# A chunk's picks within 30 slots instead of 36, and the dense gates spread over 108 slots instead of 72

## The chip, the cores and the metric

The kernel runs on one core of a Trainium2 chip. The metric is the device time of one execution in microseconds (us), lower is better. The kernel before takes 3666.66 us, the median of three runs (3649.32 to 3670.26 us).

## The reference

The program is one layer of a decoder. Its first half mixes tokens with two recurrent head groups and ends in a first layer norm. The second half, which this case is about, is PEER: each token picks 16 of 16384 experts for each of 8 heads and sums their outputs.

```
s = einsum('thcd,hckd->thck', q, keys)          # two score lists of 128 keys for each head
s1, i1 = top_k(s[:, :, 0], 16);  s2, i2 = top_k(s[:, :, 1], 16)
cand = s1[..., :, None] + s2[..., None, :]      # 256 sums, whose best 16 are the picks
top, pos = top_k(cand, 16)
eidx = take_along_axis(i1 * 128 + i2, pos);  gate = softmax(top)
hid = gelu(einsum('td,thkd->thk', x, u[eidx]))
out = einsum('thk,thkd->td', gate * hid, v[eidx])
x2 = LayerNorm(ALPHA * x1 + out)
```

There are 1024 prompt tokens in 8 chunks of 128, and 8 sample tokens that are padded to a ninth chunk. All data are float32.

## The kernel before, in words

The function `build_peer` writes out by hand the order of the instructions of each of the five engines as one loop over 656 slots (`for t in range(SLOTS)`). The engines are tied by semaphores alone.

Five chunks (0 to 4) are gathered: a slot t brings the row of `peer_u` of one pick of each of the 128 tokens with an indirect DMA of GpSimd (L1437, 512 KB), and VectorE forms the dot product of it with the token (L1707, "the dot"). 20 slots later the row of `peer_v` of the same pick is gathered in the same way (L1437) and TensorE adds it into PSUM (L2053), with gates that ScalarE writes as diagonals (L1893). So a slot is two gathers of 512 KB, one dot, and half a pair of v rows on TensorE. There are four buffers for u rows and four for v rows. GpSimd issues the gather of slot t once the dot of slot t - 4 is done. The number of a slot is the number of its dot, and the windows of the trace that stand below are cut at the starts of dots.

Three chunks (5, 6, 7) are dense. Their gates are spread into a matrix of 16384 experts by 384 tokens in DRAM, and from slot 320 (`SD`) on 128 blocks of experts are multiplied whole on TensorE (L2002, L2013, L2026), beside the rest of the gathers. Block b has its place at slot 321 + 13b/5.

Beside the slots below 320 runs the preparation of the chunks, in the order 0, 1, 5, 6, 2, 7, 3, 4, sample. `background(s)` says in which period q a slot lies and at which place `at` in it. Below slot 24 q is 0. From there a period has 36 slots: q = 1 from slot 24, q = 7 from slot 240, q = 8 in slots 276 to 311. In a period q:

- VectorE does `pick(q, ...)` in 22 steps (two lots of four heads with 11 steps each), and `norm1` of chunk q+1 in 6 steps. Four steps of a lot are `top16` over four lists of score sums of 128 keys together (L1530 to L1545), two are `top16` over 80 sums, two are the three wide operations L1596, L1600 and L1601, and the other three are short.
- TensorE does the output projection `mix` of chunk q+2 in 16 steps (L1971, two matmuls each), the transposes of chunk q+1 (L1980) and its 32 `score` steps (L1989). Before, one mix step stands in each slot from 2 to 12 and from 31 to 35, and two score steps in each slot from 15 to 30.
- ScalarE takes roots and exponentials, copies scores and the transposed chunk out of PSUM, and issues the stores of `x1`, of the transposed dense chunk and of the picks.
- The queue of SyncE loads four pieces of 256 KB of `mixT` (`load_mt`), 512 KB of `x` (`load_x`) and every 16 slots turns a set of gates (`turn_gates`). It works strictly in order, so a wait of one load holds the later ones.

The spreading of the dense gates is done in 96 quads of four tokens. A quad is four `tensor_scalar` (L1652) and one `tensor_tensor` (L1654) of VectorE that make one-hot rows, four small matmuls (L2096), and a copy by ScalarE to the tile `stag` (L1856). Every eighth quad a store of 2 MB to `gd_d` follows. Before, the quads stand in slots 246 to 317, four in three slots (`quad_slot`). The picks of the three dense chunks are transposed just ahead of them, in slots 243 to 246. They use PSUM banks 2 and 3, which the last `mix` must have left.

After slot 320 ScalarE waits with its first copy for the last quad and for all stores to `gd_d`.

Of the kernel before, what the change touches and what calls it, by code (L numbers as in the profile page):

```python
# [1067 lines left out]
def build_peer(nc, a, o, L_):  # L1068
# [12 lines left out]
    GATHERED, DENSE, SAMPLE = 5, (5, 6, 7), 8  # L1081
    ORDER = (0, 1, 5, 6, 2, 7, 3, 4, 8)
    PICK = {t: p for p, t in enumerate(ORDER)}
    NP = len(ORDER)
    ND = len(DENSE)
# [2 lines left out]
    U_SLOTS = GATHERED * CH  # L1088
    LAG, LAG_PE, SD = TOPK, TOPK + 4, 320
    PE_ROWS = SD - LAG_PE  # L1090
    SLOTS = U_SLOTS + LAG
    NBLK = NE // P
    GQ = TD // 4
# [9 lines left out]

    def background(s):

        return (0, s) if s < 24 else ((s + 12) // 36, (s + 12) % 36)

    def v_rows(t):

# [11 lines left out]
    def by_dve(v):  # L1121

        return max(0, v - PE_ROWS)

# [2 lines left out]
        return 2 * p + 2 if p else 0  # L1127

    def quad_slot(q):
        return 246 + q * 72 // GQ  # L1130

    def block_slot(b):
        return SD + 1 + b * 13 // 5
# [5 lines left out]
    with ExitStack() as ctx:  # L1139
# [103 lines left out]
        with nc.Block() as block:  # L1243
            @block.sync
            def _(sp):
# [96 lines left out]
                for t in range(SD):  # L1342
                    q, at = background(t)
                    p = q + 1
                    if at == 0 and q + 2 < NP:
                        load_mt(q + 2, 1)
                    if at == 6 and q + 2 < NP:
                        load_mt(q + 2, 2)
                    if at == 10 and q + 2 < NP:
                        load_mt(q + 2, 3)  # L1350
                    if at == 15 and p + 1 < NP:
                        load_x(p + 1)
                    if (t == 22 or at == 32) and q + 3 < NP:
                        load_mt(q + 3, 0)
                    if t in (1, 8, 15, 23):
                        load_first_gixv(t // 7)
                    if t == 64:
                        load_gix(1)
                        load_gixv(1)
                        load_x1g(1)  # L1360
                    if t == 172:
                        sp.wait_ge(s["ysum"], 1)
                        load_gix(2)
                        load_gixv(2)
                    if t == 242:
                        sp.wait_ge(s["mixg"], 4 * NP - 3)
                        for d in range(ND):
                            sp.wait_ge(s["pkst"], 16 * PICK[DENSE[d]])
                            sp.dma_start(pkd[:, d, :, :], pk_d[DENSE[d], :, 0:3, :]).then_inc(s["pkl"], 16)
                        load_x1g(2)  # L1370
                    if t == 254:
                        sp.wait_ge(s["x1"], NP)
                        wide(gb1[:, :], "ln2_g", s["gl1"])
                        wide(gb2[:, :], "ln2_b", s["gl2"])
                    if t == 274:
                        sp.wait_ge(s["sco"], 4 * NP)
                        for d in range(ND):
                            sp.wait_ge(s["xtst"], 16 * (d + 1))
                            sp.dma_start(xraw[:, :, d * CH:(d + 1) * CH], xt_d[d]).then_inc(s["xdl"], 16)
                    if t == 286:  # L1380
                        sp.wait_ge(s["ysum"], 2)
                        load_gix(3)
                    if t >= TOPK and t % TOPK == 0 and t // TOPK <= (PE_ROWS + TOPK - 1) // TOPK:
                        turn_gates(t // TOPK - 1)
                    if t == 300:
                        for b in range(3):
                            load_u(b)
                        for b in range(3):
                            load_v(b)
                    if t == 304:  # L1390
                        sp.wait_ge(s["stored"], 16)
                        load_x1g(3)
# [98 lines left out]
            def _(dve):  # L1491
# [195 lines left out]
                for t in range(SLOTS):  # L1687
                    c, h, k = t // CH, t % CH // TOPK, t % TOPK
                    q, at = background(t)
# [64 lines left out]
                            pick(0, 1 + step // 8, step % 8)  # L1754
                    if 1 <= q < NP:
                        for step in range(22):
                            if 1 + step * 34 // 21 == at:
                                pick(q, step // 11, step % 11)
                    norm_at = (1, 2, 3, 6, 7, 11) if q else (8, 9, 10, 12, 13, 15)
                    if q + 1 < NP and at in norm_at:  # L1760
                        norm1(q + 1, norm_at.index(at))

# [52 lines left out]
            def _(act):  # L1815
# [21 lines left out]
                def exp(p, part):  # L1837
                    nh = 4 if p else 2
                    hs = slice(nh * part, nh * part + nh)
                    act.wait_ge(s["top0"], parts_before(p) + part + 1)  # L1840
                    S.activation(gates_of(p)[:, hs, :], gates_of(p)[:, hs, :], ACT.Exp).then_inc(s["exp0"], 1)
# [39 lines left out]
                for t in range(SLOTS):  # L1881
                    q, at = background(t)
# [15 lines left out]
                    if q + 1 < NP:  # L1898
                        if at == (4 if q else 11):
                            root1(q + 1)  # L1900
                        if at == (12 if q else 16):
                            act.wait_ge(s["x1"], q + 2)
                            act.dma_start(x1_d[tok(ORDER[q + 1]), :], x1[:, :]).then_inc(s["x1st"], 16)
                        if at == (14 if q else 17):
                            evac_x1(q + 1)
                        if at == 16 and ORDER[q + 1] in DENSE:
                            act.wait_ge(s["x1tc"], q + 2)
                            act.dma_start(xt_d[DENSE.index(ORDER[q + 1])], x1T[:, :, :]).then_inc(s["xtst"], 16)
                        if t == 23 or at == 31:
                            evac_scores(q + 1, 0)  # L1910
                            evac_scores(q + 1, 1)
                    if t in (5, 12, 20):
                        exp(0, (5, 12, 20).index(t) + 1)
                    if t in (6, 8):
                        evac_scores(0, t // 2 - 1)
                    if 1 <= q < NP and at in (13, 31):
                        exp(q, at // 31)
                    for r in range(len(NORM2)):
                        if t - NORM2[r] == 3:
                            root2(r, mv7[:, 1:2])  # L1920
                        if t - NORM2[r] == 13:
                            store_y(r)
                    if t in (244, 245, 246):
                        d = t - 244
                        act.wait_ge(s["pkt"], d + 1)
                        S.copy(it[:, d, :, :].rearrange("p a n -> p (a n)"), PB[:, 2 + d % 2, 0:3 * HK]).then_inc(s["pkc"], 1)
                    for n in range(GQ):
# [35 lines left out]
            def _(pe):  # L1963
                def mix(p, j):
                    m = 4 * p + j // 4 - 3
                    if j % 4 == 0:
                        pe.wait_ge(s_mt[m % 2], 16 * (m // 2 + 1))
                    if j == 0:
                        free(pe, s["stt"], p)
                    for h in range(2):  # L1970
                        last = T.matmul(PB[:, 2 + h, :], mt[:, m % 2, j % 4, :], wo[:, j, h * 512:(h + 1) * 512], start=j == 0, stop=j == 15)  # L1971
                    if j % 4 == 3:
                        last.then_inc(s["mixg"], 1)
# [67 lines left out]
                for t in range(SD):  # L2041
                    q, at = background(t)
# [13 lines left out]
                    if q == 0:  # L2056
                        for j in range(16):
                            if 9 + j * 13 // 15 == t:
                                mix(2, j)
                        if t == 16:  # L2060
                            transposes(1)
                        if 18 <= t < 23:
                            for i in range(32 * (t - 18) // 5, 32 * (t - 17) // 5):
                                score(1, i)
                    else:
                        if q + 2 < NP:
                            if 2 <= at <= 12:
                                mix(q + 2, at - 2)
                            elif at >= 31:
                                mix(q + 2, at - 20)  # L2070
                        if q + 1 < NP:
                            if at == 13:
                                transposes(q + 1)
                            if 15 <= at <= 30:
                                score(q + 1, 2 * (at - 15))
                                score(q + 1, 2 * (at - 15) + 1)
                    if t in (243, 244, 245):
                        d = t - 243
                        if d == 0:
                            pe.wait_ge(s["stt"], NP)  # L2080
                            pe.wait_ge(s["pkl"], 16 * ND)
                        else:
                            free(pe, s["pkc"], d - 1)
                        pe.sem_inc(s["passed"], 1)
                        for x in range(3):
                            last = T.transpose(PB[:, 2 + d % 2, x * HK:(x + 1) * HK], pkd[:, d, x, :], ident[:, :])
                        last.then_inc(s["pkt"], 1)
# [117 lines left out]
```

## Time and profile before

| | |
|---|---|
| median of three runs | 3666.66 us |
| the profiled execution: own time | 3655.92 us |
| its span | 3653.9 us |
| mean granted TensorE clock | 0.949 |
| PE, DVE, ACT, POOL busy over the span | 89%, 71%, 23%, 48% |
| dot of slot 0, 24, 210, 318 starts at | 1079.7, 1161.1, 1793.3, 2273.5 us |

The page cuts the span into 40 slices of 91.3 us. Slots 24 to 318 lie in slices 13 to 25. The busy shares over the whole span say little here, since stages with different limits follow each other. One has to read the shares of each stretch.

### The profile page before, as it was taken

How to read it: one execution, taken by the hardware profiler on the slowest of the kernel's cores; microseconds unless marked ns; L12 is line 12 of the kernel's file. 1: busy time of each engine (PE TensorE's matmuls, PEld its weight loads, DVE VectorE, ACT ScalarE, POOL GpSimd, SP SyncE). 2: the span in 40 equal slices, each digit the busy share in tenths (PEclk: the TensorE clock that was granted, in tenths of full speed). 3: DMA queues.
4: the chain of work that ended last, by engine and by line, in shares of the span. 5: the costliest groups of instructions: out<-in, count | busy, mean ns of one | idle time of the engine just before them, and what ended most of it. 6: DMA issues, size and time to landing. Idle time of an engine off the chain costs nothing.

```text
span 3653.9 us, 46321 instructions
## 1 busy us (share of the span) xinstructions
PE 3256.1 (89%) x15535; PEld 2241.9 (61%) x15535; DVE 2610.8 (71%) x5599; ACT 831.4 (23%) x1727; POOL 1738.2 (48%) x1424
## 2 busy tenths in 40 slices
PE   6998999799988888888877656899999999999998
PEld 6998998789833223222324433577766766777765
DVE  6662000598847788888889998777777777877777
ACT  2111111465511111111113333111111111111111
POOL 2333220122203667666775566555555555555553
PEclk9999999899899999999999878899999999999999
DMA  3334333666755999999998888999999999999997
GB/s 102 87 85 144 111 127 105 234 235 226 281 208 176 345 344 348 347 335 348 364 334 289 297 298 298 396 391 383 394 390 394 393 385 381 377 400 393 396 374 247
DMA packets 392043, 1074.32 MB, mean 294 GB/s; under 512 B 57872, under 2 KB 155120, under 8 KB 384672
## 3 DMA queue, kind: packets, MB, share of 16 engines
q0 software_dynamic: 186624, 679.56, 50.0%
q1 hardware_dynamic: 132024, 298.86, 22.9%
q10 hardware_dynamic: 73192, 93.41, 7.1%
q8 instruction: 101, 1.65, 0.2%
q14 instruction: 102, 0.84, 0.1%
HBM read 978.45 MB, written 93.02 MB: 293 GB/s over the span
## 4 chain that ended last, share of the span: by engine, by line
PE 37%; DVE 13%; DMA 11%; issue 7%; POOL 4%; ACT 0%; POOLq 0%; DVEq 0%; SPq 0%; ACTq 0%
PE PB L2026 16%; PE PB L2013 13%; DMA vbf<-in_peer_v,gixv 6%; DMA x1d<-in_peer_u 3%; DVE ub L1707 3%; PE PB L2002 3%; DVE oha L1652 2%; PE PB L2053 2%; POOL ub L1437 2%; POOL vbf L1437 2%; DVE ohb L1654 1%; DMA ub<-in_peer_u,gix 1%; PE PB L1989 1%; PE PB L1971 1%; DVE work L1600 0%
## 5 line engine op out<-in xcount | busy, mean ns | idle before, releaser
L1437 POOL DMA_INDIRECT ub<-in_peer_u,gix x640 | 722.8, 1129 | 673.7 <-DVE hid L1707 477.9
L2026 PE MATMUL PB<-vbd,wd 128*128 128x512 f32 x1536 | 683.3, 595 | 0.0
L2013 PE MATMUL PB<-xds,uts 128*128 128x384 f32 x3072 | 568.4, 339 | 0.0
L2013 PEld LDWEIGHTS PB<-xds,uts 128*128 128x128 f32 x3072 | 530.7, 189 | 0.5 <-issue 0.5
L1437 POOL DMA_INDIRECT vbf<-in_peer_v,gix x340 | 396.1, 1165 | 163.9 <-issue 99.1
L1437 POOL DMA_INDIRECT vbf<-in_peer_v,gixv x300 | 353.4, 1178 | 252.0 <-PE PB L2053 121.6
L2026 PEld LDWEIGHTS PB<-vbd,wd 128*128 128x128 f32 x1536 | 283.2, 191 | 308.5 <-issue 308.5
L2053 PE MATMUL PB<-vbf,dg 128*64 128x512 f32 x1200 | 336.7, 686 | 131.8 <-DMA vbf<-in_peer_v,gixv 130.5
L1668 DVE TENSOR_TENSOR uts<-PB,uts 128x512 fp32r<-128x512 f32 x256 | 175.8, 687 | 295.6 <-ACT uts L1869 295.3
L1707 DVE CUSTOM_DVE_ANT_0 ub<-ub,x1g 128x1024 f32<-128x1024 f32 x257 | 313.6, 1222 | 78.4 <-DMA ub<-in_peer_u,gix 69.0
L1707 DVE CUSTOM_DVE_ANT_0 ub<-ub,x1gb 128x1024 f32<-128x1024 f32 x256 | 311.2, 1216 | 3.8 <-DMA ub<-in_peer_u,gix 3.5
L1869 ACT CAST uts<-PB 128x512 fp32r<-128x512 f32 x256 | 150.1, 586 | 644.1 <-PE PB L2002 631.9
L2053 PEld LDWEIGHTS PB<-vbf,dg 128*64 128x64 f32 x1200 | 90.0, 151 | 321.9 <-issue 309.2
L1746 DVE SCALAR_TENSOR_TENSOR acc<-vbf,wg,acc 128x1024 f32<-128x1024 f32 x212 | 271.2, 1279 | 5.2 <-DMA vbf<-in_peer_v,gix 4.0
L1989 PE MATMUL PB<-wp,x1T 128*128 128x512 f32 x576 | 269.3, 611 | 1.2 <-ACT x1T L1835 1.2
L1971 PE MATMUL PB<-wo,mt 128*128 128x512 f32 x528 | 248.3, 615 | 14.3 <-DVE x L1498 9.6
L270 PE MATMUL PB<-wtkh,xh 128*128 128x256 f32 (+1 forms) x864 | 244.5, 283 | 11.2 <-ACT xps L304 11.2
L967 DVE MEMSET onec<- 128x1 f32 x1 | 0.1, 59 | 345.8 <-PEq L108 345.8
L270 PE MATMUL PB<-wtkh,xl 128*128 128x256 f32 (+1 forms) x864 | 243.3, 282 | 0.0
L270 PE MATMUL PB<-wtkl,xh 128*128 128x256 f32 (+1 forms) x864 | 242.5, 281 | 0.0
L2096 PE MATMUL PB<-oha,ohb 128*128 128x128 f32 x768 | 131.5, 328 | 106.9 <-DVE ohb L1654 106.8
L2096 PEld LDWEIGHTS PB<-oha,ohb 128*128 128x128 f32 x768 | 114.2, 230 | 157.0 <-DVE ohb L1654 144.0
(399 smaller groups left out, 5340.0 us busy)
## 6 DMA issues: line engine op xcount, KB each, us to landing
vbd<-in_peer_v SPq DMA_DIRECT2D x128, 512.0 KB, 7.0
x1d<-in_peer_u SPq DMA_DIRECT2D x96, 512.0 KB, 9.3
gd_d<-stag ACTq DMA_DIRECT2D x12, 2048.0 KB, 10.1
gbd<-gd_d SPq DMA_DIRECT2D x16, 1536.0 KB, 19.0
ubd<-in_peer_u SPq DMA_DIRECT2D x32, 512.0 KB, 9.6
wtr<-in_w_tok SPq DMA_DIRECT2D x12, 1024.0 KB, 8.1
tok_d<-stg ACTq DMA_DIRECT2D x96, 128.0 KB, 1.7
rb<-rows_d SPq DMA_DIRECT2D x8, 1536.0 KB, 8.3
```

The costliest lines, as they stand in the source:

```text
L270: last = nc.tensor.matmul(PB[0:n, b, 0:TW], x[:, k, t * CH:t * CH + n], w[:, k, :], start=k == 0 and v == 0, stop=k == KD - 1 and v == 2)
L1437: pool.indirect_dma_start(out=buf, out_offset=None, in_=a[table], in_offset=bass.IndirectOffsetOnAxis(ap=index, axis=0)).then_inc(done, 16)
L1668: V.tensor_tensor(uts[:, b % 2, 1, 4 * x:4 * x + 4, :].rearrange("p k e -> p (k e)"), PB[:, 7, :], uts[:, b % 2, 0, 4 * x:4 * x + 4, :].re ...
L1707: V.tensor_tensor_reduce(out=ub[:, t % NB, :], in0=ub[:, t % NB, :], in1=by, scale=1.0, scalar=0.0, op0=ALU.mult, op1=ALU.add, accum_out=i ...
L1746: V.scalar_tensor_tensor(y, vbf[:, v % NB, :], wg[:, hv % 2, col:col + 1], y, ALU.mult, ALU.add).then_inc(s["ax"], 1)
L1869: S.copy(uts[:, b % 2, 0, 4 * x:4 * x + 4, :].rearrange("p k e -> p (k e)"), PB[:, 7, :]).then_inc(s["utc"], 1)
L1971: last = T.matmul(PB[:, 2 + h, :], mt[:, m % 2, j % 4, :], wo[:, j, h * 512:(h + 1) * 512], start=j == 0, stop=j == 15)
L1989: last = T.matmul(PB[:, 4 + n, :].rearrange("p (h n) -> p h n", h=4), x1T[:, kk, :], wp[:, 4 * n:4 * n + 4, kk, :], start=kk == 0, stop=kk ...
L2013: last = T.matmul(PB[:, 6, 0:TD], uts[:, b % 2, ul, k, :], xds[:, xl, k, :], start=(k, n) == (0, 0), stop=(k, n) == (KD - 1, 2))
L2026: last = T.matmul(PB[:, 2 * d + n, :], wd[:, b % 2, d * CH:(d + 1) * CH], vbd[b % 8][:, n * 512:(n + 1) * 512], start=b == 0, stop=b == NB ...
L2053: last = T.matmul(PB[64 * g:64 * g + 64, x, :], dg[:, n % 2, g, :], vbf[:, (v0 + g) % NB, x * 512:(x + 1) * 512], start=v0 % CH == 0, stop ...
L2096: last = T.matmul(PB[:, 2 + m % 2, x * P:(x + 1) * P], ohb[:, m % 2, x, :], oha[:, m % 2, x, :], start=True, stop=True)
```

## The change

The period becomes 30 slots (`PERIOD`), so q = 7 starts at slot 204, q = 8 at slot 234, and the preparation ends at slot 264. The 22 steps of a pick stand in slots 1 to 29 of a period. The steps of `norm1`, the roots, exponentials, copies, stores and loads get earlier places in it. The mix steps follow a list: one in each slot from 2 to 10, and seven in slots 25 to 29. The 32 score steps stand in slots 12 to 24, two or three in a slot. The work of slots below 24 stays as it was. The gates are spread from slot 210 (`SPREAD`) on, eight quads in nine slots, up to slot 316; what stood ahead of them (the loads of the dense picks, their transposes and copies) moves from slots 242 to 246 to slots 206 to 210, and the load of the second norm's weights from slot 254 to slot 216.

```diff
+    PERIOD, SPREAD = 30, 210
+    MIX_AT = (2, 3, 4, 5, 6, 7, 8, 9, 10, 25, 26, 26, 27, 28, 28, 29)
@@ background
-        return (0, s) if s < 24 else ((s + 12) // 36, (s + 12) % 36)
+        return (0, s) if s < 24 else (1 + (s - 24) // PERIOD, (s - 24) % PERIOD)
@@ quad_slot
-        return 246 + q * 72 // GQ
+        return SPREAD + q * (SD - 2 - SPREAD) // GQ
@@ SyncE
-                    if at == 15 and p + 1 < NP:
+                    if at == (13 if q else 17) and p + 1 < NP:
                         load_x(p + 1)
-                    if (t == 22 or at == 32) and q + 3 < NP:
+                    if (t == 22 or q and at == 27) and q + 3 < NP:
                         load_mt(q + 3, 0)
-                    if t == 242:
+                    if t == SPREAD - 4:
-                    if t == 254:
+                    if t == 216:
@@ VectorE
-                            if 1 + step * 34 // 21 == at:
+                            if 1 + step * 28 // 21 == at:
                                 pick(q, step // 11, step % 11)
-                    norm_at = (1, 2, 3, 6, 7, 11) if q else (8, 9, 10, 12, 13, 15)
+                    norm_at = (1, 2, 3, 5, 6, 9) if q else (8, 9, 10, 12, 13, 15)
@@ ScalarE
-                        if at == (12 if q else 16):
+                        if at == (10 if q else 16):
                             act.wait_ge(s["x1"], q + 2)
                             act.dma_start(x1_d[tok(ORDER[q + 1]), :], x1[:, :]).then_inc(s["x1st"], 16)
-                        if at == (14 if q else 17):
+                        if at == (12 if q else 17):
                             evac_x1(q + 1)
-                        if at == 16 and ORDER[q + 1] in DENSE:
+                        if q and at == 14 and ORDER[q + 1] in DENSE:
-                        if t == 23 or at == 31:
+                        if t == 23 or q and at == 22:
                             evac_scores(q + 1, 0)
                             evac_scores(q + 1, 1)
-                    if 1 <= q < NP and at in (13, 31):
-                        exp(q, at // 31)
+                    if 1 <= q < NP and at in (11, 26):
+                        exp(q, at // 26)
-                    if t in (244, 245, 246):
+                    if 0 <= t - (SPREAD - 2) < ND:
@@ TensorE
-                            if 2 <= at <= 12:
-                                mix(q + 2, at - 2)
-                            elif at >= 31:
-                                mix(q + 2, at - 20)
+                            for j in range(16):
+                                if MIX_AT[j] == at:
+                                    mix(q + 2, j)
-                            if at == 13:
+                            if at == 11:
                                 transposes(q + 1)
-                            if 15 <= at <= 30:
-                                score(q + 1, 2 * (at - 15))
-                                score(q + 1, 2 * (at - 15) + 1)
-                    if t in (243, 244, 245):
+                            for i in range(32):
+                                if 12 + i * 13 // 32 == at:
+                                    score(q + 1, i)
+                    if 0 <= t - (SPREAD - 3) < ND:
```

## Rows read from the trace of the kernel before

**Rows 1.** The page's slices of 91.3 us: VectorE and the DMA engines, in tenths.

```profile
DVE  6662000598847788888889998777777777877777
DMA  3334333666755999999998888999999999999997
```

**Rows 2.** Windows by period, q = 1 to 8; columns as in the first line.

```profile
core 0: us, PE busy (x) PEld busy (x) DVE busy (x) ACT busy (x) POOL busy (x), PEclk, DMA share, GB/s
1161.10:1297.70 136.60, 119.16 (x334) 43.30 (x335) 98.70 (x326) 22.05 (x54) 81.25 (x75) 0.95 0.82 299
1297.70:1419.70 122.00, 100.64 (x282) 35.45 (x280) 98.45 (x325) 22.11 (x55) 81.68 (x73) 0.94 0.94 342
1419.70:1534.30 114.60, 96.08 (x282) 34.21 (x280) 98.58 (x325) 20.69 (x52) 79.91 (x72) 0.97 0.96 349
1534.30:1655.10 120.80, 99.02 (x284) 34.92 (x280) 99.61 (x326) 20.94 (x53) 80.39 (x73) 0.94 0.94 337
1655.10:1770.60 115.50, 97.13 (x282) 34.48 (x280) 98.34 (x325) 19.98 (x50) 78.58 (x73) 0.97 0.97 352
1770.60:1884.10 113.50, 95.80 (x282) 34.18 (x280) 98.23 (x324) 21.40 (x53) 79.46 (x71) 0.98 0.96 350
1884.10:2058.50 174.40, 124.74 (x545) 67.43 (x541) 167.06 (x533) 61.10 (x95) 95.90 (x74) 0.86 0.85 301
2058.50:2247.10 188.60, 118.63 (x528) 72.67 (x528) 183.38 (x567) 67.87 (x99) 111.08 (x78) 0.78 0.82 292
```

**Rows 3.** Windows of slots 24-210, 210-318, 264-318, and of 333-640.

```profile
1161.10:1793.30 632.20, 529.71 (x1504) 188.31 (x1503) 513.86 (x1706) 110.74 (x272) 417.24 (x379) 0.96 0.92 336
1793.30:2273.50 480.20, 338.93 (x1391) 179.03 (x1391) 448.55 (x1394) 154.83 (x247) 291.09 (x220) 0.85 0.86 308
1999.80:2273.50 273.70, 181.21 (x818) 109.65 (x818) 260.88 (x785) 100.18 (x145) 159.90 (x111) 0.80 0.83 296
2350.60:3574.40 1223.80, 1212.49 (x5211) 859.40 (x5210) 943.87 (x1312) 199.04 (x381) 689.74 (x616) 1.00 1.01 388
```

**Rows 4.** Who waited for whom, 1222 to 1793 us: total, times, longest.

```profile
PE PB L2053 <- DMA vbf<-in_peer_v,gixv: 88.7, 71, 6.1
DVE ub L1707 <- DMA ub<-in_peer_u,gix: 71.8, 62, 4.3
```

**Rows 5.** DMA view: the gathers' queue from 1297.7 to 1884.1 us.

```profile
q0 software_dynamic: 51883, 188.90, 88.2%
```

**Rows 6.** Groups by line in period 5, 1655.1 to 1770.6 us: VectorE, TensorE.

```profile
L1707 DVE CUSTOM_DVE_ANT_0 ub<-ub,acc 128x1024 f32<-128x1024 f32 x37 | 45.3, 1228 | 16.3 <-DMA ub<-in_peer_u,gix 14.1 <-DVE idx L1545 0.9 <-DVE pos L1545 0.7
...
L1707 DVE DVE_READ_ACCUMULATOR2_ANT hid<- 128x1 f32 x36 | 3.0, 82 | 0.0
...
L2053 PE MATMUL PB<-vbf,dg 128*64 128x512 f32 x146 | 38.7, 649 | 17.0 <-DMA vbf<-in_peer_v,gixv 17.0
L1971 PE MATMUL PB<-wo,mt 128*128 128x512 f32 x64 | 29.8, 606 | 1.3 <-DVE x L1498 1.3
L1989 PE MATMUL PB<-wp,x1T 128*128 128x512 f32 x64 | 29.7, 607 | 0.0
```

**Rows 7.** Windows of the three thirds (12 slots each) of period 5.

```profile
1655.10:1694.10 39.00, 30.82 (x93) 10.84 (x90) 35.14 (x136) 6.29 (x16) 25.92 (x24) 1.00 0.98 355
1694.10:1735.60 41.50, 34.71 (x99) 12.28 (x98) 33.89 (x107) 7.84 (x19) 26.00 (x26) 0.92 0.95 343
1735.60:1770.60 35.00, 31.61 (x93) 11.37 (x93) 29.31 (x83) 5.86 (x15) 26.66 (x24) 1.00 0.98 359
```

**Rows 8.** VectorE's timeline around one quad: start, us, instruction.

```profile
2016.00 1.11 DVE L1652 TENSOR_SCALAR oha<-iof,it 128x128 f32<-128x128 f32 x4
2017.03 0.68 DVE L1654 TENSOR_TENSOR ohb<-iof,it 128x512 f32<-128x512 f32 x1
2017.63 1.10 DVE L1652 TENSOR_SCALAR oha<-iof,it 128x128 f32<-128x128 f32 x4
```

**Rows 9.** DMA view, issues of slots 264 to 318: the stores of gates.

```profile
gd_d<-stag ACTq DMA_DIRECT2D x9, 2048.0 KB, 9.5
```

**Rows 10.** The chain that ended last: its piece at slots 318 to 320.

```profile
2275.97 13.99 DMA gd_d<-stag
```

More of the change, by code:

```diff
@@ L1922, in _ @@
                             store_y(r)
-                    if t in (244, 245, 246):
-                        d = t - 244
+                    if 0 <= t - (SPREAD - 2) < ND:
+                        d = t - (SPREAD - 2)
                         act.wait_ge(s["pkt"], d + 1)
@@ L2066, in _ @@
                         if q + 2 < NP:
-                            if 2 <= at <= 12:
-                                mix(q + 2, at - 2)
-                            elif at >= 31:
-                                mix(q + 2, at - 20)
+                            for j in range(16):
+                                if MIX_AT[j] == at:
+                                    mix(q + 2, j)
                         if q + 1 < NP:
-                            if at == 13:
+                            if at == 11:
                                 transposes(q + 1)
-                            if 15 <= at <= 30:
-                                score(q + 1, 2 * (at - 15))
-                                score(q + 1, 2 * (at - 15) + 1)
-                    if t in (243, 244, 245):
-                        d = t - 243
+                            for i in range(32):
+                                if 12 + i * 13 // 32 == at:
+                                    score(q + 1, i)
+                    if 0 <= t - (SPREAD - 3) < ND:
+                        d = t - (SPREAD - 3)
                         if d == 0:
```

## The prediction

> **What bounds the kernel now.** I read the page's slices first. The change lies in slots 24 to 318, slices 13 to 25. There the digits of the two trade places: in slices 14 to 21 the DMA engines are at 9 and VectorE at 7 or 8, in slices 22 to 24 VectorE is at 9 and the DMA engines at 8 [rows 1]. The windows by period say it in numbers. Periods 2 to 6 take 122.0, 114.6, 120.8, 115.5 and 113.5 us (mean 117.3) at a DMA share of 0.94 to 0.97, with VectorE busy for 98.5 of them; periods 7 and 8, which hold the quads, take 174.4 and 188.6 us with VectorE busy for 167.1 and 183.4, that is 0.96 and 0.97 of the time, and the DMA share is 0.85 and 0.82 [rows 2]. The waits of the first part are waits for gathered rows, 88.7 us on TensorE and 71.8 us on VectorE [rows 4]. So slots 24 to 246 are bound by the DMA engines and slots 246 to 318 by VectorE. From slot 333 on TensorE is busy for 1212 of 1224 us [rows 3]; nothing of the change is there.
>
> The reader is to see what this leaves to win. VectorE's work moves out of a stretch that it bounds into one where it has 16% to spare, and where the DMA engines have 4% to spare. The DMA engines' own work over slots 24 to 318 is 0.92 x 632.2 + 0.86 x 480.2 = 995 us of 1112.4 [rows 3]. At the share of 0.96 that periods 2 to 6 hold, that is 1036 us. 76 us is the most that any placing of steps gives.
>
> **Part 1, periods of 30 slots (slots 24 to 210).** No operation is removed. Slots 24 to 210 held 5.2 periods and now hold 6.2. I work out one period by three engines.
>
> - DMA: the share times the time, averaged over periods 2 to 6, is 112 us [rows 2]. The gathers take 88.2% of 586.4 us for 180 slots, 2.87 us a slot [rows 5]. Six slots fewer leave 112 - 17 = 95 us.
> - VectorE: 98.5 us, less six dots of (45.3 + 3.0)/37 = 1.31 us [rows 6], is 90.6. Where VectorE was the bound it was busy for 0.965 of the time [rows 2], so its bound is 94 us.
> - TensorE: period 5 has 97.1 us, less six slots of 38.7/36 = 1.08 us [rows 6], is 91 us.
>
> Three engines within 5% of each other don't run at once at 100%, so the halves of a period matter. In slots 0 to 11 of a period seven steps of `pick` become nine; the two that come in are the short one and one of the three wide operations, about 5 us. Today these 12 slots take 39.0 us, with VectorE busy for 35.1 (36.4 at 0.965) and the DMA share at 0.98 [rows 7]. So VectorE asks 41.5 us there and becomes the bound: 42 us. In the 18 slots left TensorE has 18 x 1.08 = 19.4 us of v rows, all scores (29.7) and 7 of 16 mix steps (13.0) [rows 6], 62 us; the DMA engines have 95 - 39 = 56, over 0.96 58 us. 42 + 62 is 104 us. The four buffers let one half run a little into the other: I take 103 us. The ends are 98 (DMA at 0.96 alone) and 112 (62 us of TensorE at a lower clock, below).
>
> Period 1 takes 136.6 us with TensorE busy for 119.2 [rows 2]. It is TensorE's already, and six slots fewer take 1.08 to 1.5 us each from it: 128 us. Period 6 is today 4 us below the mean, so 101 less 0 to 3 us; I take 101, which with 103 for the others is on the high side. The first six slots of period 7 now belong here. They hold five steps of `pick` and most of `norm1`, as slots 240 to 245 do: 23 us, 3.9 us a slot, a bit above the 3.25 (39.0/12) of a period's first third [rows 7]. The sum is 128 + 4 x 103 + 101 + 23 = 664 us against 632.2: **+32 us**.
>
> **Part 2, the stretch with picks and quads (slots 210 to 264).** A quad is 2017.63 - 2016.00 = 1.63 us of VectorE [rows 8]. Here are 48 quads (78 us), 54 dots (70.5), 1.8 periods of picks and norm (98.5 - 36 x 1.31 = 51.4 each, 92.5, less 5 us since period 8 has no `norm1`) and half a second norm (3 us): 239 us busy, over 0.97 **246 us**, 4.6 us a slot. The DMA engines need less: 0.86 x 480.2 = 413 us for slots 210 to 318, of which 209 fall to part 3, 204 here. TensorE has in slots 216 to 228 1.08 of v rows, 32/13 scores of 29.7/32 = 2.3 us, and a quad's matmuls of about 1 us, 4.4 us a slot: covered by VectorE at full clock, 2 to 5 us late at the 0.86 of period 7 [rows 2].
>
> **Part 3, quads without picks (slots 264 to 318).** VectorE has 54 dots (70.5), 48 quads (78) and 10 us of norms: 159 us, 2.9 a slot. It is no longer the bound. What is late next is the DMA: its work is 0.83 x 273.7 = 227 us [rows 3], less three of the nine stores of gates [rows 9], since 48 quads are left of 72. A store of 2.1 MB takes 5.9 us at the 357 GB/s (296/0.83) of the stretch, so 227 - 18 = 209 us, over 0.96 **218 us**. The ends are 159 (VectorE) and 230 (share 0.91). Parts 2 and 3 together are 464 us against 480.2: **-16 us**. Only 16 us of VectorE's relief is left, because the same gathers and stores must pass.
>
> **Part 4, the hand-over to the blocks.** The chain waits 13.99 us for the last store of gates [rows 10]. The last quad is one slot earlier and its store starts that much earlier: **-4 us** (0 to -8). The loads that moved to slots 206 and 216 keep their distance to what uses them; `load_x` at slot 13 waits for the store of slot 10 as it waited at 15 for the store of 12, and behind it on SyncE's queue stand only pieces of `mixT` and the turned gates, which are needed four slots later. I cost them at nothing; they are worth 0 to +5 us if that cover is gone.
>
> The sum is 32 - 16 - 4 = +12 us on the profiled execution's 3655.92 us (its span is 3653.9): **3668 us**. The median shown is 3666.66, 11 us above that execution, so 3668 by this reckoning is a little slower than the same kernel's profiled execution and cannot be told from its median. A difference of 0.5% is 18 us, about what a measurement of this kernel can tell from no change.
>
> The Trainium skill's page Perfetto Trace Analysis, Optimization Strategy, says that a kernel whose most-contended engine changes over time may gain from interleaving those regimes. By that rule the moved quads would fill VectorE's idle time and the stretch would come near to its DMA work; the sum would be rival B's. The rows speak for only part of it, since the regime into which the work goes has 4% left on the DMA engines and TensorE within 5% of it [rows 2].
>
> **Rivals.**
>
> - **B, the DMA engines have more left than their share says.** In slots 333 to 640 they move 388 GB/s [rows 3], in part 3 357 GB/s at full share. If part 3 moves its 81.0 - 6.3 = 74.7 MB at 388, it takes 193 us instead of 218, and periods 2 to 6 come to 99 and 98 us (DMA at 0.96) instead of 103 and 101: 12 - 25 - 16 - 3 = -32, **3624 us**. For it: the first third of a period already runs VectorE at 0.93 with the DMA share at 0.98 [rows 7], so nearness of two bounds costs little. Against: every window of slots 60 to 240 stays at 337 to 352 GB/s [rows 2], with the same gathers. The Trainium skill's page DMA: Bandwidth & Descriptors, Where 436 GB/s comes from, puts the HBM side of a core at about 358 GB/s. By that rule B couldn't be, but the 388 GB/s of slots 333 to 640 don't agree with it, so I give it no weight.
> - **C, TensorE becomes the bound of slots 12 to 29, and its clock falls.** All scores now wait for one copy of the transposed chunk at slot 12, then 62 us of work stand in 18 slots. In the second third of period 5, where TensorE waits for that copy, the granted clock is 0.92 between two thirds at 1.00, and it is the longest third, 41.5 us [rows 7]. If the clock is 0.90 over those 18 slots instead of 0.96, they take 66 us and a period 108: 5 us more in each of periods 2 to 6 and 2 us in period 7, +27, **3695 us**. It decides from about 63 us on TensorE for those slots. Against: busy time on TensorE has modelled ends, and more work beside it may keep the clock up.
>
> **How the numbers follow.** The forecast has 0.52 (own range 3640 to 3690: 0.02 faster, 0.37 same, 0.13 slower), B 0.22 (0.18 faster, 0.04 same), C 0.26 (0.24 slower, 0.02 same). That gives 0.20 faster by over 0.5%, 0.43 within, 0.37 slower. The range goes from B's 3624 to a little over C's 3695: 3625 to 3703.
>
> **What would show it.** Period 3 (now slots 84 to 114) should take 103 us, with VectorE at about 0.88 and the DMA share at about 0.92; 98 or 99 speaks for B, 108 for C. Slots 12 to 29 of a period should be longer than 58 us, with TensorE busy. Slots 210 to 264 should take 246 us with VectorE at 0.97, and slots 264 to 318 218 us with VectorE near 0.73 and DMA at 0.96. If that last stretch takes 200 us or less, the DMA term was wrong; if the first takes over 680 us, part 1 was. From slot 333 on nothing should differ by over 5 us.

## The result

The changed kernel takes 3678.88 us (median of 15 runs, 3659.64 to 3688.35) against 3661.55 us for the kernel before in the same set (15 runs, 3647.57 to 3670.76). The ratio of all these runs is 1.0036, 95% interval 1.0021 to 1.0051: slower by 13 us, less than 0.5% (the medians alone differ by 17 us). The forecast was +12 us on one execution. That is nearly the measured difference, and by luck: part 1 was forecast 22 us too long, parts 3 and 4 13 and 7 us too short. These steps are what is worth reading.

In the profile after, the page's slices show the trade. VectorE is now at 9 in slices 16 to 22 (before, of the slices 13 to 25 it was so in 22 to 24 only) and drops to 8, 6 and 5 in slices 23 to 25; the dip of the DMA engines to 7 and 8 is still there, from slice 21 instead of 22 on [rows 1].

```profile
DVE  6661000588847889999999865777777777877777
DMA  3334333666755999999978888999999999999997
```

The windows by period of 30 slots (1 to 6), then slots 204 to 210, 210 to 264, 264 to 318, 318 to 320 and 333 to 640, with the columns of [rows 2]:

```profile
1166.20:1285.60 119.40, 107.80 (x304) 40.11 (x302) 90.96 (x315) 20.27 (x48) 69.76 (x63) 0.97 0.81 291
1285.60:1388.30 102.70, 90.51 (x260) 32.55 (x260) 91.27 (x314) 18.82 (x46) 66.60 (x62) 0.97 0.95 342
1388.30:1485.70 97.40, 90.17 (x258) 32.27 (x258) 90.92 (x314) 18.95 (x46) 66.00 (x60) 0.96 0.96 349
1485.70:1585.20 99.50, 88.73 (x256) 32.16 (x252) 90.79 (x312) 18.93 (x46) 66.80 (x60) 0.98 0.95 345
1585.20:1687.30 102.10, 90.63 (x263) 32.70 (x264) 92.18 (x315) 18.34 (x46) 70.21 (x62) 0.98 0.93 335
1687.30:1784.40 97.10, 86.27 (x252) 31.34 (x248) 90.81 (x313) 17.86 (x44) 65.37 (x59) 1.00 0.95 347
1784.40:1808.40 24.00, 12.98 (x46) 4.38 (x45) 20.38 (x85) 6.77 (x16) 14.26 (x14) 0.86 0.91 325
1808.40:2056.10 247.70, 165.87 (x664) 85.98 (x664) 235.99 (x779) 74.77 (x120) 144.69 (x109) 0.79 0.81 283
2056.10:2287.10 231.00, 133.39 (x602) 70.58 (x602) 158.30 (x366) 67.15 (x110) 155.68 (x112) 0.78 0.90 325
2287.10:2306.90 19.80, 6.54 (x26) 2.32 (x22) 3.11 (x6) 2.34 (x5) 5.89 (x7) 0.67 0.98 373
2367.50:3597.40 1229.90, 1214.98 (x5211) 860.89 (x5210) 943.14 (x1312) 199.29 (x381) 692.17 (x616) 0.99 1.00 386
```

| slots | before, us [rows 3] | forecast, us | after, us |
|---|---|---|---|
| 24 to 210 | 632.2 | 664 | 642.2 |
| 210 to 264 | 206.5 | 246 | 247.7 |
| 264 to 318 | 273.7 | 218 | 231.0 |
| 318 to 333 | 77.1 | 73 | 80.4 |

The sum over these slots is +11.8 us. (Slots 210 to 264 before are 480.2 less 273.7.) The span of this execution is 3676.9 us against 3653.9, 23 us more: 5 of the other 11 lie ahead of slot 24 and 6 behind slot 333, where nothing was changed. The other profiled executions of this study start slot 0 anywhere between 1079.7 and 1088.7 us and take 1217.1 to 1233.0 us for slots 333 to 640, so that part is within the scatter. Stretches scatter too: e4 below does in slots 264 to 318 the same work as the changed kernel and takes 228.0 us for them, not 231.0.

### The profile page after: what moved, and what is told of

Its sections match the earlier page's. It is cut to its first block, busy times and chain, and to the rows that moved or that the text cites. A ratio compares the mean times of both kernels' runs of the same rounds, so it can differ in the third digit from the quotient of the medians.

```text
span 3676.9 us, 46320 instructions
## 1 busy us (share of the span) xinstructions
PE 3263.9 (89%) x15535; PEld 2242.9 (61%) x15535; DVE 2612.3 (71%) x5599; ACT 828.2 (23%) x1725; POOL 1747.4 (48%) x1424
## 4 chain that ended last, share of the span: by engine, by line
PE 41%; DVE 13%; DMA 10%; issue 5%; POOL 3%; ACT 0%; DVEq 0%; POOLq 0%; ACTq 0%; SPq 0%
PE PB L2028 16%; PE PB L2015 13%; DMA vbf<-in_peer_v,gixv 5%; DVE ub L1709 4%; PE PB L1991 4%; DMA x1d<-in_peer_u 3%; PE PB L2055 3%; PE PB L2004 3%; DVE oha L1654 1%; PE PB L1973 1%; POOL ub L1439 1%; DMA ub<-in_peer_u,gix 1%; POOL vbf L1439 1%; DVE ohb L1656 1%; DVE work L1602 0%
## 5 line engine op out<-in xcount | busy, mean ns | idle before, releaser
L1439 POOL DMA_INDIRECT ub<-in_peer_u,gix x640 | 738.4, 1154 | 666.4 <-DVE hid L1709 455.6
L2055 PE MATMUL PB<-vbf,dg 128*64 128x512 f32 x1200 | 348.5, 708 | 169.2 <-DMA vbf<-in_peer_v,gixv 147.9
L1709 DVE CUSTOM_DVE_ANT_0 ub<-ub,x1gb 128x1024 f32<-128x1024 f32 x256 | 311.7, 1218 | 55.3 <-DMA ub<-in_peer_u,gix 55.0
L1709 DVE CUSTOM_DVE_ANT_0 ub<-ub,x1g 128x1024 f32<-128x1024 f32 x257 | 312.7, 1221 | 51.6 <-DMA ub<-in_peer_u,gix 43.5
L270 PE MATMUL PB<-wtkl,xh 128*128 128x256 f32 (+1 forms) x864 | 242.5, 281 | 0.0
L1991 PEld LDWEIGHTS PB<-wp,x1T 128*128 128x128 f32 x576 | 106.3, 192 | 160.6 <-issue 152.7
L1973 PEld LDWEIGHTS PB<-wo,mt 128*128 128x128 f32 x528 | 98.7, 195 | 165.0 <-issue 165.0
```

Of the source, the lines that this page charges most:

```text
L270: last = nc.tensor.matmul(PB[0:n, b, 0:TW], x[:, k, t * CH:t * CH + n], w[:, k, :], start=k == 0 and v == 0, stop=k == KD - 1 and v == 2)
L1439: pool.indirect_dma_start(out=buf, out_offset=None, in_=a[table], in_offset=bass.IndirectOffsetOnAxis(ap=index, axis=0)).then_inc(done, 16)
L1709: V.tensor_tensor_reduce(out=ub[:, t % NB, :], in0=ub[:, t % NB, :], in1=by, scale=1.0, scalar=0.0, op0=ALU.mult, op1=ALU.add, accum_out=i ...
L1991: last = T.matmul(PB[:, 4 + n, :].rearrange("p (h n) -> p h n", h=4), x1T[:, kk, :], wp[:, 4 * n:4 * n + 4, kk, :], start=kk == 0, stop=kk ...
L2055: last = T.matmul(PB[64 * g:64 * g + 64, x, :], dg[:, n % 2, g, :], vbf[:, (v0 + g) % NB, x * 512:(x + 1) * 512], start=v0 % CH == 0, stop ...
```

## The experiments

All are made from the changed kernel but e7. Each diff shows the main lines of its edit. The windows below are in the order of their slots, with the columns of [rows 2]. e3, e4, e6 and e9 ran once each, so their times have no interval, and their stretches are compared with those of one execution.

**e1, the first part alone.** The quads go back to slots 246 to 317. The load of `x1g(2)` stays at slot 206, with a wait of its own.

```diff
-    PERIOD, SPREAD = 30, 210
+    PERIOD, SPREAD = 30, 246
@@ SyncE
+                    if t == 206:
+                        sp.wait_ge(s["mixg"], 4 * NP - 3)
                         load_x1g(2)
```

> The first part of the change alone: periods of 30 slots, the quads back in slots 246 to 317 (72 slots, 1.33 quads a slot); the load of x1g(2) goes by itself at slot 206, with the wait for the last mix. Theory (each stretch goes by its slowest engine, and the DMA engines reach a share of 0.90 where 2 MB stores run): slots 24 to 210 stay at 642 us; 210 to 246 are picks without quads, 115 us; 246 to 264 are 18 slots of picks and 24 quads, 93 us by VectorE; 264 to 318 hold 72 quads, VectorE 198 us, DMA 227 us over 0.90 = 252 us. In all slots 210 to 318 460 us against 478.7 of the changed kernel: 0.5% faster than it, ratio to the kernel before 0.998 to 1.001. Rival 1 (the second part of the change is what helps, and without it the kernel is slower still): 1.008 or more. Rival 2 (VectorE alone sets slots 264 to 318): they take 205 us, ratio 0.990.

Measured: 3652.41 us (12 runs), ratio to the kernel before 0.9985 (0.9967 to 1.0002). Slots 24-210, 210-246, 246-264 and 264-318:

```profile
1167.30:1813.00 645.70, 567.02 (x1621) 204.54 (x1619) 567.58 (x1957) 118.33 (x283) 412.21 (x378) 0.97 0.92 332
1813.00:1932.50 119.50, 84.45 (x225) 27.20 (x225) 105.51 (x368) 21.90 (x54) 77.50 (x71) 0.72 0.93 329
1932.50:2027.40 94.90, 56.19 (x256) 35.39 (x256) 91.55 (x291) 31.27 (x47) 48.97 (x39) 0.77 0.74 256
2027.40:2269.90 242.50, 155.94 (x794) 92.24 (x794) 196.39 (x486) 91.75 (x135) 177.54 (x113) 0.82 0.92 340
```

Slots 210 to 318 take 457 us where 460 were expected (119.5, 94.9 and 242.5 us for 115, 93 and 252). So the second part of the change, spreading the gates over 108 slots, costs 22 us here (478.7 less 457), and it is what made the whole slower. Half as many quads again (72 for 48) lengthen slots 264 to 318 by only 11.5 us.

**e2, all quads behind the picks.** The load of `x1g(2)` is as in e1.

```diff
-    PERIOD, SPREAD = 30, 210
+    PERIOD, SPREAD = 30, 262
```

> As e1, but all 96 quads stand behind the picks, in slots 262 to 317 (1.71 a slot). Theory: slots 210 to 264 by VectorE without quads 171 us (3.2 a slot); slots 264 to 318 VectorE 237 us over 0.97 = 244, DMA (227 + 18) over 0.90 = 272 us; together 443 us, 36 us below the changed kernel, ratio to the kernel before 0.993 to 0.996. Rival 1 (the quads cost least where they are thin): slower than the changed kernel, 1.008. Rival 2 (VectorE alone): 415 us, ratio 0.986.

Measured: 3624.24 us (6 runs), ratio 0.9907 (0.9879 to 0.9934), faster than both kernels. Slots 24-210, 210-264, 264-318:

```profile
1161.10:1803.80 642.70, 567.01 (x1619) 204.10 (x1618) 567.34 (x1958) 118.26 (x283) 411.85 (x377) 0.97 0.92 332
1803.80:1990.10 186.30, 117.21 (x320) 38.23 (x321) 164.66 (x558) 33.20 (x80) 123.82 (x111) 0.74 0.92 326
1990.10:2235.50 245.40, 173.41 (x957) 112.94 (x955) 230.07 (x587) 114.03 (x155) 189.47 (x111) 0.91 0.94 349
```

Slots 210 to 318 take 431.7 us, 48.5 below before and 47 below the changed kernel. Nearly twice the quads in slots 264 to 318 (92 for 48) cost 14 us. The DMA share is 0.92 and 0.94 now, where it was 0.81 and 0.90. The expectation had 272 us for the last stretch, 245 us of DMA work over a share of 0.90. Both were off: the work is 0.94 x 245.4 = 231 us, and the share rose with the load. VectorE is busy for 230 of these 245 us, also 0.94, and its own term of the expectation, 244 us, is what was measured. Which of the two binds there was not tested.

**e3, half the dots.** The dots of slots below 320 run over 512 of 1024 columns, so the hidden values of the gathered chunks lack half of their sum.

```diff
+                        w = D // 2 if t < SD else D
-                        V.tensor_tensor_reduce(out=ub[:, t % NB, :], in0=ub[:, t % NB, :], in1=by,
+                        V.tensor_tensor_reduce(out=ub[:, t % NB, 0:w], in0=ub[:, t % NB, 0:w], in1=by[:, 0:w],
```

> The changed kernel with the dots of slots below 320 over half the columns (the hidden values of the gathered chunks are wrong): VectorE gets 0.5 us a slot, 16 us a period, back, and nothing else changes. If the DMA engines and TensorE are as near to the bound of a period of 30 slots as VectorE, periods 2 to 6 fall only from 100.4 to 96 to 98 us. If VectorE alone bounds them they fall to 88 or less. Slots 210 to 264 (VectorE's) fall from 248 to the DMA's 204/0.93 = 220 us. Slots 264 to 318: no change from 231 (228 to 234) if gathers and stores bound them; 205 if VectorE does.

Measured: 3620.84 us (one run). Slots 54 to 204 by period, then 210-264 and 264-318:

```profile
1280.90:1380.70 99.80, 89.12 (x258) 32.16 (x257) 75.22 (x312) 18.86 (x45) 61.41 (x61) 0.98 0.97 353
1380.70:1478.50 97.80, 89.09 (x258) 31.99 (x257) 75.18 (x312) 18.86 (x45) 62.44 (x61) 0.98 0.96 346
1478.50:1575.90 97.40, 87.87 (x259) 31.95 (x257) 75.39 (x311) 18.95 (x45) 62.54 (x61) 1.00 0.96 355
1575.90:1676.30 100.40, 89.24 (x264) 32.23 (x264) 76.48 (x313) 18.12 (x44) 61.69 (x61) 1.00 0.95 343
1676.30:1768.90 92.60, 84.89 (x250) 30.95 (x247) 75.57 (x313) 18.12 (x45) 60.36 (x59) 1.00 0.97 357
1792.30:2015.70 223.40, 159.92 (x662) 84.08 (x664) 207.40 (x778) 74.40 (x121) 136.87 (x110) 0.81 0.88 316
2015.70:2235.80 220.10, 134.34 (x606) 70.85 (x604) 129.53 (x366) 67.05 (x110) 132.14 (x112) 0.79 0.92 340
```

(The 100.4 of the expectation is the mean of periods 2 to 5; with period 6 it is 99.8.) VectorE has 16 us a period less, and periods 2 to 5 shorten by 1.5 us, to 98.9; period 6 shortens by 4.5 us. So VectorE is not what bounds periods 2 to 5, and e4 will say the same of TensorE. What is left is the DMA engines, busy for 0.96 of the time; no run takes work from them there, so that is shown by exclusion only. Slots 210 to 264 lose 24 us; they were VectorE's. Slots 264 to 318 lose 11 us (8 against e4), where none was expected. This need not be VectorE's own time: GpSimd's instructions, which issue the gathers, get shorter too, and it is busy for 132 us in place of 156 (see the last section).

**e4, fewer scores.** 5 of 8 matmuls of each score from the third chunk on, so the scores and with them the picks are others.

```diff
-                    last = T.matmul(PB[:, 4 + n, :]..., start=kk == 0, stop=kk == KD - 1)
+                    if kk < KD // 2 or p < 2 and kk < KD - 1:
+                        T.matmul(PB[:, 4 + n, :]..., start=kk == 0, stop=False)
+                    if kk == KD - 1:
+                        last = T.matmul(PB[:, 4 + n, :]..., start=False, stop=True)
```

> The changed kernel with 5 of the 8 matmuls of each score for chunks from the third on (the scores and so the picks are wrong, the number of gathers is the same): TensorE gets 12 x 0.86 = 10 us a period back in slots 12 to 24. By the prediction's step (TensorE bounds slots 12 to 29 with 62 us) periods 2 to 6 fall from 100.4 to 94 to 96 us. If that step was wrong (slots 12 to 29 took 55.5 us, near VectorE's own 53) they stay at 99 to 101. Slots 264 to 318 don't change.

Measured: 3679.80 us (one run). Periods 2 to 5 take 104.3, 96.5, 100.7 and 101.2 us, mean 100.7. Nothing changed. Slots 96 to 114 and 126 to 144 (places 12 to 29 of periods 3 and 4), first of the changed kernel:

```profile
1431.40:1485.70 54.30, 53.05 (x151) 19.35 (x151) 51.01 (x168) 8.71 (x22) 37.82 (x33) 1.00 0.97 353
1529.90:1585.20 55.30, 51.73 (x146) 19.06 (x146) 50.86 (x167) 9.42 (x25) 34.04 (x32) 1.00 0.95 343
```

and of e4:

```profile
1429.60:1482.90 53.30, 43.91 (x125) 15.40 (x124) 50.78 (x168) 8.58 (x22) 36.19 (x33) 0.97 0.97 353
1527.30:1583.60 56.30, 45.27 (x127) 15.77 (x125) 50.96 (x166) 9.85 (x26) 37.16 (x34) 0.97 0.96 347
```

TensorE is busy for 53.1 of 54.3 us, 98%, in the changed kernel. Taking 9 us of it away in the first of these windows, and 6 in the second, leaves the times within 1 us of what they were. A busy share of 98% on TensorE was no bound. Slots 264 to 318, which the edit doesn't touch:

```profile
2055.20:2283.20 228.00, 133.29 (x600) 70.97 (x600) 155.49 (x367) 67.06 (x110) 148.21 (x112) 0.79 0.92 328
```

**e6, the subtractions on VectorE.** Four subtractions stand between the gathers on GpSimd in slots 290 to 296.

```diff
-                        nc.gpsimd.tensor_tensor(xds[:, 1, 2 * k:2 * k + 2, :], ...   # in GpSimd's loop
+                        V.tensor_tensor(xds[:, 1, 2 * k:2 * k + 2, :], ...           # in VectorE's loop
```

> The changed kernel with the four subtractions 128x768 of slots 290 to 296 on VectorE instead of GpSimd, where they stand between gathers. Slots 288 to 294 took 33.4 us, their neighbours 25. Theory: GpSimd's 4 x 1.85 us hold back the gathers, and with them on VectorE (4 x 0.8 us in idle time) slots 288 to 294 take 25 to 27 us and slots 264 to 318 fall from 231 to 223. Rival: those slots are long because of the three loads of 512 KB and a store of 2 MB that are in flight there; then slots 264 to 318 stay at 229 to 233.

Measured: 3669.76 us (one run). Slots 288-294, 294-300 and 264-318:

```profile
2157.80:2190.10 32.30, 12.81 (x52) 7.06 (x54) 18.50 (x43) 8.00 (x13) 18.34 (x13) 0.68 0.98 369
2190.10:2209.70 19.60, 14.78 (x78) 7.88 (x74) 16.85 (x40) 7.31 (x12) 13.52 (x10) 0.92 0.87 298
2060.90:2286.60 225.70, 124.71 (x598) 68.57 (x600) 155.69 (x370) 67.38 (x110) 142.56 (x107) 0.79 0.92 332
```

Slots 288 to 294 took 33.4 us in the changed kernel and take 32.3; the DMA share is 0.98 there, so they are long by the bytes in flight and not by the subtractions. Slots 294 to 300 fall from 25.3 to 19.6. The whole stretch is 5 us shorter, between the two expectations, but only 2 us shorter than in e4, whose subtractions are where they were. So a gain was not shown; that GpSimd's subtractions cost up to 5 us stays a possibility.

**e7, late quads without the first part.** The kernel before, periods of 36 slots, with the quads in slots 262 to 317; what stands ahead of them moves by 16 slots, the load of `x1g(2)` stays at slot 242.

```diff
-        return 246 + q * 72 // GQ
+        return 262 + q * 56 // GQ
```

> The kernel before (periods of 36 slots) with the quads in slots 262 to 317 instead of 246 to 317, as e2 has them; the transposes and copies ahead of them move with them. Theory: where picks and quads share slots VectorE is the bound and only its sum counts, so slots 210 to 262 get faster (3.2 us a slot, 166 us) and slots 262 to 318 slower (5.5 us of VectorE over 0.97, 318 us): 484 us against 480, ratio to the kernel before 0.998 to 1.004. What made e2 fast is then that periods of 30 slots free slots 264 to 318 of picks for all quads. Rival: late quads are good in themselves: 0.990 to 0.994 as in e2.

Measured: 3667.41 us (10 runs), ratio 1.0022 (0.9998 to 1.0046). Slots 24-210, 210-262, 262-318:

```profile
1170.20:1797.80 627.60, 530.33 (x1502) 188.29 (x1501) 514.09 (x1706) 110.83 (x272) 415.99 (x378) 0.95 0.93 337
1797.80:1968.70 170.90, 127.29 (x363) 43.83 (x363) 141.49 (x453) 31.46 (x76) 113.34 (x103) 0.88 0.94 343
1968.70:2285.40 316.70, 210.18 (x1033) 135.81 (x1029) 308.42 (x941) 124.86 (x169) 167.86 (x119) 0.84 0.81 284
```

170.9 + 316.7 = 487.6 us, where 484 were expected, and 480.2 is the kernel before. Where picks and quads share slots, VectorE is busy for 0.97 of them, and how they are shared out gains nothing. Neither late quads alone (1.0022) nor short periods alone (e1, 0.9985) make a difference that stands clear of its interval; both together make 0.9907.

**e8, stores in halves.** e2 with each 2 MB store of gates as two of 1 MB, the second three quads later.

```diff
-                        act.dma_start(gd_d[g], stag[:, g % 2, :, :]...).then_inc(s_gst[g % 2], 16)
+                        act.dma_start(gd_d[g, :, 0:2048], stag[:, g % 2, 0:64, :]...).then_inc(s_gst[g % 2], 16)
+                    if q % 8 == 2 and g or q == GQ - 1:
+                        h = g - 1 if q < GQ - 1 else g
+                        act.dma_start(gd_d[h, :, 2048:4096], stag[:, h % 2, 64:128, :]...).then_inc(s_gst[h % 2], 16)
```

> e2 (periods of 30, quads in slots 262 to 317) with each 2 MB store of the gates issued as two halves of 1 MB, the second three quads later (the last one at once). If the bursts of the stores empty the four gather buffers, slots 264 to 318 fall from 245 to 238 to 242 us and the ratio to the kernel before goes from 0.991 to 0.989; if only the bytes count, or VectorE (230 of 245 us busy) is now the bound, no change: 0.990 to 0.992.

Measured: 3624.24 us (10 runs), ratio 0.9911 (0.9886 to 0.9936), the same as e2. Its slots 264 to 318 take 242.1 us, 3 less, which no interval supports. Bursts of stores are not what is left.

**e9, an eighth of the stores.** Only the columns of 16 of 128 blocks are stored, and the block stage reads these again and again, so the gates of the dense chunks are wrong.

```diff
-                        act.dma_start(gd_d[g], stag[:, g % 2, :, :]...).then_inc(s_gst[g % 2], 16)
+                        act.dma_start(gd_d[g, :, 0:512], stag[:, g % 2, 0:16, :]...).then_inc(s_gst[g % 2], 16)
```

> The changed kernel with an eighth of each 2 MB store of the gates: only the columns of 16 of 128 blocks are stored, and the loads of gates in the block stage read those again and again at their old size (the dense chunks are wrong; the number of stores, loads and waits is the same). It asks why slots 264 to 318 take 231 us at a DMA share of 0.90 and not 218 at 0.96. If these slots wait for the bytes of the stores, six stores less seven eighths give 6 x 5.9 x 7/8 = 31 us of DMA time back: 231 falls to about 200 (195 to 205), and slots 210 to 264 (VectorE's, 248 us) stay. If the stretch hangs on something else (GpSimd's gather instructions held up by VectorE's one-hot operations, or the chain between buffers), it stays above 215 with a DMA share near 0.82. The wait for the last store in slot 319 (17 us) shrinks by 8 to 12 us.

Measured: 3640.77 us (one run). Slots 210-264, 264-318 and 318-320:

```profile
1806.90:2050.80 243.90, 161.50 (x669) 85.17 (x670) 235.67 (x779) 75.01 (x121) 147.77 (x109) 0.82 0.74 250
2050.80:2259.00 208.20, 127.96 (x600) 69.37 (x598) 160.78 (x366) 66.94 (x110) 153.73 (x111) 0.83 0.88 306
2259.00:2272.70 13.70, 5.94 (x22) 2.74 (x20) 3.11 (x6) 2.40 (x5) 7.92 (x8) 0.75 0.95 361
```

231.0 falls to 208.2, 23 us of the 31 (20 us against e4), and 3 us short of the range expected. The DMA work falls from 0.90 x 231 = 208 to 0.88 x 208.2 = 183 us, so 25 us less work gave 23 us less time: the stretch waits for the bytes, at a share that hardly moves. Slots 210 to 264, whose stores shrink as well, lose only 4 us at a DMA share of 0.74, so they are not the DMA engines'. Slots 318 and 319 get 6 us shorter. (e5, the same cut with the rest of the gates left unwritten, gave no time.)

## Why the prediction was right, and where it was not

**What bounds what** held. Slots 210 to 264 were to be VectorE's at 246 us with 0.97 busy; they take 247.7 with 0.95, and e3 gives 24 us back, e9 only 4. In slots 264 to 318 the bytes set most of the time, as was forecast: e9 says so.

**Part 1, the period** (+32 forecast, +10 measured). The DMA term was right: 95 us, measured 0.95 x 99.8 = 95. Period 3 takes 97.4 us and not 103, with VectorE at 0.93 and the DMA engines at 0.96. The step that failed is "in the 18 slots left TensorE has ... 62 us", added to the 42 us of the other 12 slots. These 18 slots take 53.3 to 58.2 us in periods 2 to 6 (54.3 and 55.3 in the rows under e4), and e4 shows that TensorE isn't even their bound. TensorE's groups in them, period 3:

```profile
L1991 PE MATMUL PB<-wp,x1T 128*128 128x512 f32 x61 | 27.9, 603 | 0.0
L2055 PE MATMUL PB<-vbf,dg 128*64 128x512 f32 x66 | 16.1, 605 | 1.2 <-DMA vbf<-in_peer_v,gixv 1.2
L1973 PE MATMUL PB<-wo,mt 128*128 128x512 f32 x24 | 10.8, 601 | 0.0
```

These are 151 matmuls, and the step had added up 72 + 64 + 28 = 164. At the busy time of one in these rows all 164 are 59 us, so 3 us of the 62 were the price. The other 13 ran in the slots on either side, where TensorE is busy for only 37 of 43 us: the halves of a period don't end at the same slot on each engine, and bounds of two engines in two halves can't be added as if they did. That cost 10 us over periods 2 to 5 and 4 in period 6.

Period 1 was to be TensorE's too ("it is TensorE's already"), so six slots were to take 1.08 to 1.5 us each from it. They took 136.6 - 119.4 = 17.2 us, 2.87 each. That is also the price of a slot's gathers [rows 5], though no run tests whether that is the reason. Period 1 so came out 8.6 us shorter than forecast. In e4 the last 18 slots of period 1 take 56.6 us against 55.9, with 7.9 us less of TensorE's work, so TensorE isn't their bound. What sets the first 12, which take 63.5 us, stays open.

VectorE's bound in places 0 to 11 was near: 42 us forecast, 43.1 to 45.4 measured in periods 2 to 6. But e3 shortens these slots of periods 2 to 5 from 44.3 to 41.1 us on average and lengthens the other 18 from 56.1 to 57.7. What one half gives back the other mostly takes, which fits a period that is bound by the DMA engines as a whole.

**Part 3, slots 264 to 318** (218 forecast, 231 measured). The DMA work was sized right, 209 us against 208. What failed is the divisor: the share of 0.96 was taken from stretches without 2 MB stores and without quads, and it is 0.90 here (0.92 in e4). The stores and quads by themselves don't explain it, since e2 and e8, which have more of both there, hold 0.94 and 0.95. Half dots make the stretch 8 to 11 us shorter (e3), through VectorE or through GpSimd's instructions; moved subtractions 2 to 5 us (e6), no more than scatter. The cause of the lower share stays open.

**Part 4, the hand-over** (-4 forecast, +3.3 measured). The last quad did stand a slot earlier, but its store did not leave earlier. The chain of waits of the changed kernel at that place:

```profile
2279.31 5.82 DMA vbf<-in_peer_v,gixv
2285.26 3.28 PE PB L2055 x8
...
2290.75 14.78 DMA gd_d<-stag
2308.18 4.67 issue
```

TensorE works in order, and the quad's matmuls stood behind a pair of v rows that had waited for its gather. The store left 3.7 us behind the dot of slot 318, and 2.5 us behind it before [rows 10]. So the slot of a step in such a stretch doesn't fix its time; the transfer that the step stands behind does.

**Rival C** (a lower clock in places 12 to 29) fell: the granted clock is 1.00 in four of these five windows, as in the two rows under e4, and in e4 itself 0.94 to 0.97 without costing time. The Trainium skill's page Perfetto Trace Analysis, section Identifying the Most-Contended Engine, says that matmul busy time is a poor measure of how near TensorE is to its limit. The trace agrees, 98% busy and no bound in e4; the page's reason, that pipelined instructions look smaller than they are, would make the share read too low, while here it read too high. **Rival B** (388 GB/s) fell too: slots 264 to 318 move 325 GB/s, and at most 349 in e2 and 353 in e8. Its times for the periods did come, 100.4 us for periods 2 to 5 and 97.1 for period 6 where it had 99 and 98, but at 335 to 349 GB/s: they are the DMA work over a share of 0.95, not a higher rate.

**The rule weighed ahead**, of the Trainium skill's page Perfetto Trace Analysis, Optimization Strategy (interleave regimes with different bounds), gave less than nothing as the change applied it, and 0.9907 as e2 does. The difference is where the idle time of VectorE is. The change put half of the quads into slots 210 to 264, which the picks of 30 slots had already filled (VectorE 0.95 busy), and left slots 264 to 318 with VectorE at 0.69. I had worked out both numbers, 246 us at 4.6 us a slot and 2.9 us of VectorE a slot behind it, and didn't draw the conclusion that the quads belonged behind the picks.

## What to carry to other kernels

Before work is spread thinner, look which slots it is spread into: add up each engine's work for each stretch, and put it where the engine that does it is idle, not where the schedule is long. In e2 the same change with one number other, 262 for 210 (and one load by itself), is 1.3% faster than the change as it was made (0.9907 against 1.0036). Don't add the bounds of two engines in two parts of a period: here the sum was 103 us and the period 97 to 103, mean 100, near the 99 of one engine's work over the whole period. The DMA engines' share times the time gave their own work within 1 us twice, and in e2's expectation 14 us too much. Don't count a move by a single slot as time where the step waits behind a transfer.

## What the runs showed of the hardware

GpSimd's gather instruction takes longer the more VectorE does beside it. Its mean for u rows in slots 264 to 318, with 48, 72 and 92 quads there (changed kernel, e1, e2), and with 48 quads and half dots (e3):

```profile
L1439 POOL DMA_INDIRECT ub<-in_peer_u,gix x54 | 77.1, 1427 | 15.9 <-issue 15.4 <-PE PB L2055 0.3
L1441 POOL DMA_INDIRECT ub<-in_peer_u,gix x54 | 84.1, 1558 | 17.5 <-issue 15.3 <-DVE hid L1711 2.3
L1441 POOL DMA_INDIRECT ub<-in_peer_u,gix x53 | 94.8, 1789 | 22.4 <-issue 13.7 <-DVE hid L1711 7.8 <-PE PB L2057 0.9
L1439 POOL DMA_INDIRECT ub<-in_peer_u,gix x54 | 62.6, 1160 | 15.9 <-issue 14.4 <-PE PB L2056 1.2 <-DVE hid L1710 0.3
```

In periods 2 to 6, without quads, the mean is 1129 ns. Two gathers of 1.72 us and 0.3 us of issue each are 4.0 us of the 4.5 us a slot of e2, so GpSimd is close behind VectorE and the DMA engines there.

Which instruction does it can be read from the timeline of the changed kernel. A gather beside the four `tensor_scalar` of a quad (L1654) takes 0.94 us; one that starts in the `tensor_tensor` of a quad (L1656), with a dot (L1709) behind it, takes 2.47:

```profile
2076.78 1.14 DVE L1654 TENSOR_SCALAR oha<-iof,it 128x128 f32<-128x128 f32 x4 [3.29 <-issue]
2076.86 0.94 POOL L1439 DMA_INDIRECT ub<-in_peer_u,gix  x1 [0.30 <-issue]
2242.47 0.68 DVE L1656 TENSOR_TENSOR ohb<-iof,it 128x512 f32<-128x512 f32 x1
2242.63 2.47 POOL L1439 DMA_INDIRECT ub<-in_peer_u,gix  x1 [0.30 <-issue]
2243.08 1.21 DVE L1709 CUSTOM_DVE_ANT_0 ub<-ub,x1gb 128x1024 f32<-128x1024 f32 x1
```

It is so throughout these slots. Of the 108 gathers there, the 24 with next to nothing of VectorE beside their first 0.94 us take 937 ns on average, the 8 with `tensor_scalar` alone 940, and the 25 with a `tensor_tensor` and a dot 2179 (2423 in e2, where these are 38 of 107). So it is not the count of quads as such, but how often a gather meets a `tensor_tensor` and then a dot; both read two tiles. The Trainium skill's page SBUF — State Buffer, section SBUF: two separate sides, says that a VectorE instruction with two inputs in SBUF excludes a GpSimd instruction that reads SBUF, and the other way round, for its whole length. The gather reads its rows' numbers from the tile `gix`. The trace agrees: 2.47 us is 0.94 and 1.53, and the dot ends 1.66 us after the gather's start. The `tensor_scalar`, with one tile of data, show nothing like it.
